# One expert item reordered, its gather in turned form, tables and a norm row loaded earlier, one refill in halves

## What is computed

```
h = x + token_mixer(rmsnorm(x), w_in, ..., w_out)    # attention, 8 heads; mLSTM, 4 heads
xt = rmsnorm(h, norm_ffn_w)
logits = xt @ w_router + b_router                    # 32 experts
top_val, top_idx = top_k(logits, 4); gate = softmax(top_val)
# for each expert e and the tokens that chose it (sorted into rows):
hdn = xb @ w_mlp1[e] + b_mlp1[e]                     # 1024 -> 2048
glu = min(hdn[:, :1024], 7); lin = clip(hdn[:, 1024:], -7, 7)
act = glu * sigmoid(1.702 * glu) * (lin + 1)
y = act @ w_mlp2[e] + b_mlp2[e]                      # 1024 -> 1024
out = rmsnorm(h + sum over 4 of gate * y, norm_final_w)
```

## Time and profile before

| | us |
|---|---|
| median of 3 runs | 1120.61 (1120.59 to 1120.95) |
| the profiled execution's own time | 1120.7 |
| its span, first to last instruction | 1118.7 |
| PE busy | 1081.9 (97%) |
| weight loads (PEld) busy | 485.3 (43%) |
| DVE busy | 368.2 (33%) |
| ACT busy | 246.9 (22%) |
| DMA | 439.15 MB, mean 393 GB/s |
| TensorE's granted clock | 0.998 of full speed |

### The profile page before, as it was taken

How to read it: one execution, slowest core, us unless ns; L and a number is a source line. 1 busy time by engine, 2 the same in 40 slices (tenths; PEclk the granted TensorE clock), 3 DMA queues, 4 the chain that set the end, 5 groups by cost and what they waited for, 6 DMA issues and landing times.

```text
span 1118.7 us, 14432 instructions
## 1 busy us (share of the span) xinstructions
PE 1081.9 (97%) x5393; PEld 485.3 (43%) x5394; DVE 368.2 (33%) x813; ACT 246.9 (22%) x346; POOL 3.0 (0%) x12
## 2 busy tenths in 40 slices
PE   9999999999999999999999999999999999999996
PEld 8888888533333333333333333333333333333332
DVE  6987786422222122222222222222222222222223
ACT  6745674311111111111111111111111111111112
POOL 0000000000000000000000000000000000000000
PEclk9999999999999999999999999999999999999999
DMA  9654479999999999999999999999999999999996
GB/s 337 230 186 152 151 221 421 427 412 427 428 428 435 431 429 432 433 430 432 432 431 396 431 431 432 433 433 433 431 431 431 433 431 431 431 431 431 424 424 277
DMA packets 38165, 439.15 MB, mean 393 GB/s; under 512 B 5276, under 2 KB 5464, under 8 KB 22424
## 3 DMA queue, kind: packets, MB, share of 16 engines
q1 hardware_dynamic: 37776, 437.78, 93.5%
q10 hardware_dynamic: 360, 0.95, 0.3%
HBM read 437.67 MB, written 1.05 MB: 392 GB/s over the span
## 4 chain that ended last, share of the span: by engine, by line
PE 80%; DMA 13%; DVE 6%; issue 1%; SPq 0%; ACT 0%; DVEq 0%; PEldq 0%
PE bank L1161 35%; PE bank L1190 18%; DMA ring<-in_w_mlp_dram 11%; PE bank L806 9%; PE bank L1088 3%; PE bank L1172 2%; PE bank L800 2%; DMA late_slots<-in_w_mlp_dram 2%; PE bank L968 2%; PE bank L1016 2%; DVE xn L1678 2%; DVE xn L1675 2%; DVE xn L1682 2%; PE bank L1064 1%; PE bank L1072 1%; PE bank L1138 1%
## 5 line engine op out<-in xcount | busy, mean ns | idle before, releaser
L1161 PE MATMUL bank<-ring,xn 128*64 128x512 f32 x1232 | 276.3, 595 | 6.3 <-DMA ring<-in_w_mlp_dram 6.3
L1161 PE MATMUL bank<-late_slots,xn 128*64 128x512 f32 x880 | 197.3, 595 | 3.6 <-DMA late_slots<-in_w_mlp_dram 3.5
L1161 PEld LDWEIGHTS bank<-ring,xn 128*64 128x64 f32 x1232 | 84.6, 136 | 163.6 <-issue 150.1
L1190 PE MATMUL bank<-ring,smo 128*64 128x512 f32 x624 | 138.3, 595 | 0.0
L713 ACT ACTIVATE xn<-bank 128x512 f32<-128x512 f32 x33 | 19.8, 599 | 479.9 <-PE bank L1161 479.9
L1161 PEld LDWEIGHTS bank<-late_slots,xn 128*64 128x64 f32 x880 | 60.4, 136 | 116.1 <-issue 106.5
L1691 DVE SCALAR_TENSOR_TENSOR moe_y_lo<-bank,st,moe_y_hi 128x512 fp32r<-128x512 f32 x33 | 24.8, 751 | 235.9 <-ACT moe_y_hi L720 235.9
L1675 DVE TENSOR_SCALAR xn<-bank 128x512 f32<-128x512 f32 x33 | 22.8, 692 | 219.4 <-PE bank L1161 219.4
L1190 PE MATMUL bank<-late_slots,smo 128*64 128x512 f32 x416 | 92.4, 595 | 0.2 <-DMA late_slots<-in_w_mlp_dram 0.2
L1190 PEld LDWEIGHTS bank<-ring,smo 128*64 128x64 f32 x624 | 43.0, 137 | 81.0 <-issue 81.0
L720 ACT ACTIVATE moe_y_hi<-bank,st 128x512 fp32r<-128x512 f32 x33 | 22.7, 687 | 234.1 <-PE bank L1190 234.1
(11 more groups left out here) (271 smaller groups left out, 886.3 us busy)
## 6 DMA issues: line engine op xcount, KB each, us to landing
ring<-in_w_mlp_dram SPq DMA_DIRECT2D x43, 4096.0 KB, 30.2
late_slots<-in_w_mlp_dram SPq DMA_DIRECT2D x29, 4096.0 KB, 27.8
ring<-in_w_mlp_dram SPq DMA_DIRECT2D x28, 2048.0 KB, 13.2
late_slots<-in_w_mlp_dram SPq DMA_DIRECT2D x15, 2048.0 KB, 15.3
ring<-in_w_in_dram SPq DMA_DIRECT2D x22, 1024.0 KB, 5.6
late_slots<-in_w_mlp_dram SPq DMA_DIRECT2D x6, 1024.0 KB, 35.9
ring<-in_w_branch_dram SPq DMA_DIRECT2D x4, 1024.0 KB, 5.0
ring<-in_w_out_dram SPq DMA_DIRECT2D x4, 1024.0 KB, 7.3
```

The costliest lines, as they stand in the source:

```text
L1161: last = mm(B[4 + u][g * C:(g + 1) * C, :], xgT[:, k % 4, k // 4, :], by_group(held[k // 2][0][:, k % 2, u * FF:(u + 1) * FF], g), start=F ...
L1190: last = mm(B[7][g * C:(g + 1) * C, :], actT[:, j, h * C:(h + 1) * C], held[4 + h][0][:, j // 2, (j % 2) * D + g * N:(j % 2) * D + (g + 1) ...
```

## The change

- Gather in turned form: x's columns are now the stationary operand (128 tokens by 128 features, every fourth feature), and the one-hot matrix the moving one (64 columns), so that the result comes out turned; 16 matmuls instead of 4. ACT's copy and `turn_rows` go.
- The expert item: in the last chunk of mlp1 both glu halves come first, and the new counter `glu_done` lets ACT's sigmoid and DVE's product of sigmoid and glu start before the linear half is done. DVE then clips the linear part and multiplies. `slots_used` goes up by 1 per slot instead of 2 per chunk.
- The one-hot matrix that is turned (`own`) and the identity beside it (`turner`) are bf16; the gates stand beside the identity in three bf16 pieces, made once by five DVE steps.
- b_mlp2 is issued by ACT after the copy of the slice mv, b_mlp1 and the final norm's row after the second softmax; the row has its own place in SBUF, over constants that are used no more. The constants are reordered for that.
- The first refill chunk that goes to place 0 is loaded in two halves, each when its slot is free.
- SP's wait ahead of the last quarter of w_out names `hi_used` in place of `slots_used`.

```diff
                 for t in range(TT):
                     pe.wait_ge(onehot, ready - 1 + t)
-                    for g in range(2):
-                        last = mm(B[6][g * C:(g + 1) * C, :], oneh[:, t, :], xs[:, t, g * N:(g + 1) * N],
-                                  start=(t == 0), stop=(t == TT - 1), skip_group_check=True)
+                    for j in range(ROWS):
+                        for g in range(2):
+                            rows_of = xs[:, t, g * N:(g + 1) * N].rearrange("p (q s) -> p s q", s=ROWS)[:, j, :]
+                            last = mm(B[6][:, (2 * j + g) * C:(2 * j + g + 1) * C], rows_of, oneh[:, t, :],
+                                      start=(t == 0 and j == 0 and g == 0), stop=(t == TT - 1), skip_group_check=True)
                 last.then_inc(gath, 1)
...
+                wide = P + TT * PIECES
                 for t in range(TT):
-                    last = mm(B[7][:, t * (P + TT):(t + 1) * (P + TT)], gated[:, t, :], cst[:, K_ID:K_ID + P + TT],
-                              start=True, stop=True)
+                    last = mm(B[7][:, t * wide:(t + 1) * wide], own[:, t, :], turner[:, :], start=True, stop=True)
                 last.then_inc(gt_turned, 1)
-
-            def turn_rows(ready):
-
-                pe.wait_ge(xg_out, ready)
-                for j in range(4):
-                    last = nc.tensor.transpose(B[6][:, j * P:(j + 1) * P], xg[:, j * P:(j + 1) * P], ident)
-                last.then_inc(xg_turned, 1)
...
+                def mlp1(k, u):
+                    for g in range(2):
+                        last = mm(B[4 + u][g * C:(g + 1) * C, :], xgT[:, k % 4, k // 4, :],
+                                  by_group(held[k // 2][0][:, k % 2, u * FF:(u + 1) * FF], g),
+                                  start=False, stop=(k == KB - 1), skip_group_check=True)
+                    return last
...
+                    mlp1(2 * c, 0)
+                    mlp1(2 * c, 1).then_inc(slots_used, 1)
+                    if c in in_pieces:
+                        pe.wait_ge(*in_pieces[c])
+                    mlp1(2 * c + 1, 0)
+                    mlp1(2 * c + 1, 1).then_inc(slots_used, 1)
+                pe.wait_ge(held[3][1], held[3][2])
+                mlp1(KB - 2, 0)
+                if 3 in in_pieces:
+                    pe.wait_ge(*in_pieces[3])
+                mlp1(KB - 1, 0).then_inc(glu_done, 1)
+                mlp1(KB - 2, 1)
+                if 3 in in_halves:
+                    pe.wait_ge(*in_halves[3])
+                mlp1(KB - 1, 1).then_inc(slots_used, 2)
                 gather(2 * i + 4)
...
-                turn_rows(i + 2)
                 pe.wait_ge(actT_a, i + 1)
 ...
             with act.Fori(0, items) as i:
-                act.wait_ge(slots_used, i * PER_EXPERT + (Q_MOE + KB))
+                act.wait_ge(glu_done, i + 1)
                 nc.scalar.activation(sig, B[4][:, :], ACT.Sigmoid, scale=ALPHA).then_inc(sig_ready, 1)
-                take_xg(i + 2)
                 act.wait_ge(turned_b, i + 1)
 ...
+                dve.wait_ge(sig_ready, i + 1)
+                v.tensor_scalar(sig, sig, SIG_TOP, None, ALU.min).then_inc(act_step, 1)
+                dve.wait_ge(act_step, 3 * i + 1)
+                v.scalar_tensor_tensor(out=lin, in0=B[4][:, :], scalar=LIMIT, in1=sig, op0=ALU.min, op1=ALU.mult)\
+                 .then_inc(act_step, 1)
                 dve.wait_ge(slots_used, i * PER_EXPERT + (Q_MOE + KB))
-                v.tensor_scalar(lin, B[5][:, :], LIMIT + 1.0, 1.0 - LIMIT, ALU.min, ALU.max).then_inc(lin_ready, 1)
...
+                v.tensor_scalar(B[5][:, :], B[5][:, :], LIMIT + 1.0, 1.0 - LIMIT, ALU.min, ALU.max).then_inc(act_step, 1)
+                dve.wait_ge(act_step, 3 * i + 3)
                 for j in (0, 2):
...
+                    v.tensor_tensor(actv.rearrange("p (s q) -> p q s", s=ROWS)[:, :, j:j + 2],
+                                    B[5][:, :].rearrange("p (q s) -> p q s", s=ROWS)[:, :, j:j + 2],
+                                    lin.rearrange("p (q s) -> p q s", s=ROWS)[:, :, j:j + 2], ALU.mult).then_inc(act_ready, 1)
 ...
+            v.tensor_copy(gate3[:, :, :, 0], gate[:, :, :]).then_inc(count_step, 1)
+            dve.wait_ge(count_step, 11)
+            v.tensor_tensor(gate_rest[:, :, :], gate[:, :, :], gate3[:, :, :, 0], ALU.subtract).then_inc(count_step, 1)
 ...
+            act.wait_ge(scored, AH)
+            for part in range(PIECES):
+                act.dma_start(b1raw[part * E:(part + 1) * E, :], b_mlp1[0]).then_inc(b1_in, 16)
+            act.dma_start(wfin[:, :], norm_final_w.rearrange("(a d) -> a d", a=1).broadcast_to([P, D])).then_inc(s_small2, 16)
             split(22)
...
+                elif CHUNKS * e + i == HALVED:
+                    for k in range(2):
+                        sp.wait_ge(slots_used, after * PER_EXPERT + (Q_MOE - PER_EXPERT + k + 1))
+                        sp.dma_start(places[place][:, k, :], src[:, k * SLOT:(k + 1) * SLOT]).then_inc(place_landed[place], 16)
...
-                sp.wait_ge(slots_used, min(Q_OUT + j - MIX_RING + 1, Q_BRANCH))
+                if j < 3:
+                    sp.wait_ge(slots_used, Q_OUT + j - MIX_RING + 1)
+                else:
+                    sp.wait_ge(hi_used, Q_BRANCH)
```

More of the change, by code:

```diff
@@ L123, in landings @@
             continue
-        counts[place] += 1
+        counts[place] += 2 if m == HALVED else 1
         table.append((place, counts[place]))
@@ L243, in build @@
         ohT = nc.alloc_sbuf_tensor_at("one_hot_T", [P, TT, P], F32R, offset=hm_at + 4 * S)
+        own = nc.alloc_sbuf_tensor_at("own_slots", [P, TT, P], BF16, offset=hm_at + 4 * 3 * S)
+        turner = nc.alloc_sbuf_tensor_at("ident_and_gates", [P, P + TT * PIECES], BF16, offset=hm_at + 4 * 3 * S + 2 * TT * P)
         b2t = sb("b2t", [P, N])
@@ L433, in _ @@
             for i in range(CHUNKS - 1):
-                wait_freed(after, i)
                 m = PLACES + 1 + i
+                if m != HALVED:
+                    wait_freed(after, i)
                 load(m // CHUNKS, m % CHUNKS, i)
@@ L746, in _ @@
             mm = nc.tensor.matmul
-            tables = cst[:, K_MASK:K_MASK + S]
+            tables = cst[:, K_LOWER:K_LOWER + S]
             def keep_warm(n, table, idle=B[7][:, 0:S]):
@@ L1142, in item @@
                 pe.wait_ge(xg_ready, i + 1)
-                for k in range(KB):
-                    if k == 2:
+                def mlp1(k, u):
+                    for g in range(2):
+                        last = mm(B[4 + u][g * C:(g + 1) * C, :], xgT[:, k % 4, k // 4, :],
+                                  by_group(held[k // 2][0][:, k % 2, u * FF:(u + 1) * FF], g),
+                                  start=False, stop=(k == KB - 1), skip_group_check=True)
+                    return last
+                for c in range(3):
+                    if c == 1:
                         pe.wait_ge(gT_ready, i + 1)
@@ L1150, in item @@
                         scatter(y_lo)
-                    if k == 4:
+                    if c == 2:
                         turn_gates(3 * i + 5)
-                    if k % 2 == 0:
-                        pe.wait_ge(held[k // 2][1], held[k // 2][2])
-                    elif k // 2 in in_pieces:
-                        pe.wait_ge(*in_pieces[k // 2])
-                    for u in range(2):
-                        if u and k == KB - 1 and 3 in in_halves:
-                            pe.wait_ge(*in_halves[3])
-                        for g in range(2):
-                            last = mm(B[4 + u][g * C:(g + 1) * C, :], xgT[:, k % 4, k // 4, :],
-                                      by_group(held[k // 2][0][:, k % 2, u * FF:(u + 1) * FF], g),
-                                      start=False, stop=(k == KB - 1), skip_group_check=True)
-                    if k % 2:
-                        last.then_inc(slots_used, 2)
+                    pe.wait_ge(held[c][1], held[c][2])
+                    mlp1(2 * c, 0)
[13 more added lines that the diff above has]
+                mlp1(KB - 1, 1).then_inc(slots_used, 2)
                 gather(2 * i + 4)
@@ L1558, in _ @@
                     v.memset(ohT[:, :, :].bitcast(F32), 0.0).then_inc(gated_zero, 1)
+                    v.tensor_copy(turner[:, 0:P], ident).then_inc(gated_zero, 1)
                 if n == 0:
@@ L1658, in _ @@
                 for t in range(TT):
-                    v.tensor_scalar(gated[:, t, :].rearrange("p (g s) -> p g s", g=2),
+                    v.tensor_scalar(own[:, t, :].rearrange("p (g s) -> p g s", g=2),
                                     places.unsqueeze(1).broadcast_to([P, 2, C]), at[t], None, ALU.is_equal)\
                      .then_inc(gated_ready, 1)
-                v.tensor_copy(cst[:, K_GATE:K_GATE + TT], gate[:, :, bass.ds(e, 1)].rearrange("p t a -> p (t a)"))\
-                 .then_inc(gated_ready, 1)
+                v.tensor_copy(turner[:, P:P + TT * PIECES].rearrange("p (t c) -> p t c", c=PIECES),
```

(8 more changed lines are left out.)

63 lines of the change are left out of this document (29 added, 34 removed).

## The result

The changed kernel takes 1334.45 us (median of 4 runs, 1324.23 to 1340.04) against 1120.78 for the kernel before on the same chip: a ratio of 1.189 (95% interval 1.185 to 1.193). The direction was forecast; the forecast of 1132.5 is 202 us too low, and its range ended at 1141. The profiled execution took 1339.21 us, its span 1337.3.

A forecast was written before the change was run, and what follows sets the result against it. The prediction took the later of two clocks, DMA transfers or PE, to bound the kernel. PE's 0.5 + 33 x 0.71 - 11.7 = +12.2 us on 1120.7 gave 1132.9, rounded to 1132.5; range 1117 to 1141.

The forecast's parts named there:

- Price of a pair, strided: Turned gather: each f32 pair of weight load and matmul costs 0.11 us, 32 pairs per item.
- rival C: Gather: reading every fourth column as weights is slower, 0.12 to 0.13 us a pair; about +25 us, 1146; chance 0.08.
- d: Expert item: its added length, +0.71 us forecast; 32p - 2.81, with p the time of one pair in the gather.
- The clock is no part of it: Whole kernel: TensorE ran at its full 2.4 GHz in every window, so clock speed was given no cost.
- the way from the gather's end to mlp2: Expert item: activation transposes, their copy and a semaphore before mlp2's first load, 0.95 us.
- One-hot turning: Expert item: turning the one-hots in bf16 instead of f32 saves 0.27 us, bounds 0.2 and 0.45.
- DVE's work after the last chunk: End of mlp1: clip and product, some 1.2 us, lie hidden under the gather's 3.4 us.
- s: First expert item: its start comes 0.5 us later, bounds 0 to 1.2.
- Two clocks: Kernel's end: the later of transfers (s + 14d, +10.4 us) and PE (s + 33d - 11.7, +12.2 us) decides.
- Order of chunk 3: Last chunk of mlp1: glu-first order and earlier sigmoid change the item by 0 us.
- Rival A: Gather: loads hidden, a pair costs 0.05 to 0.08 us, kernel faster at 1117.5 us; chance 0.14.
- B: Expert item: terms cancel, a pair at 0.085 to 0.09 us, kernel at 1121 us; chance 0.06.

The follow-up runs named there:

- e1: The changed kernel with 128 neighbouring columns of x as the gather's weights instead of every fourth; 1132.71 us, ratio 1.0101.
- e4: The changed kernel with the old gather back (4 matmuls, ACT's row copy, row transposes), the rest of the change kept; 1119.51 us, ratio 0.9986.
- e10: The changed kernel with contiguous gather weights and the gather done in two passes of 32 moving columns each; 1405.33 us.
- e8: The changed kernel with the gather's weights read at steps of 12, 24 and 16 bytes, the last from two starting points; 1314.72 us.
- e3: The changed kernel with strided weights kept, but 256 moving columns instead of 64 behind each load; 1306.67 us.
- e9: The changed kernel with contiguous gather weights and the gather done twice over, 64 pairs with 64 moving columns each; 1279.81 us.
- e2: The changed kernel with the gather's four weight sources read at steps of 4, 8, 16 and 32 bytes; 1248.34 us.
- e5: The kernel before with only the turned gather put in, its weights read at every fourth column; 1354.71 us.

## Why the prediction was wrong, by its steps

**Price of a pair, strided: the step that failed.** It was taken from loads of contiguous columns and carried over to a read that "as weights is in no row". That was rival C, and C had its mechanism right and its price wrong: 0.12 to 0.13 us where it is 0.239. No row bounded it from above, so the cost had to be called open, with both ends kept for the range; a range that ended at 1141, a pair of 0.118 us, had no ground. By the prediction's own d = 32p - 2.81, p = 0.239 gives d = 4.84, and PE's clock 0.5 + 33 x 4.84 - 11.7 = +148.5: 1269. The section of the Trainium skill quoted above spoke for C with its two hits in a line and against C with f32 strided by 4 for free, and the prediction weighed neither. Its remark that this stride costs nothing as moving operand has no row either: no matmul of the kernel before moves every fourth column. The gather moves 512 neighbours, and mlp1 moves four neighbours and skips four.

**"The clock is no part of it": failed for the changed kernel.** It was true of the rows of before and was never asked of the new gather. Against e1, the changed kernel's span is 206.6 us longer: 34 gathers x (7.66 - 3.71) = 134 for the loads; 33 x (8.70 - 7.09 for mlp2, + 0.20 for the transposes) = 60 and 2 in the first chunk for the clock; 10.6 for the interruption, less 1.4 that e1 waits for a transfer. Together 205. So of the forecast's 202 us of error, the loads are about two thirds and the clock three tenths.

**The rest held in the main, as e1 shows.** Pair 0.116 (forecast 0.11), so 3.71 us for 32 instead of 3.52; the way from the gather's end to mlp2 0.74 (0.24 + 0.44 and two short gaps, forecast 0.95). One-hot turning 0.64 to 0.22, so -0.42 (forecast -0.27, inside its bounds). The gather's part is then 0.62 + 0.42 = +1.04 (forecast +0.98), d = 27.38 - 26.76 = 0.62 (0.71). DVE's work after the last chunk is covered: the activation's transposes follow the gather at once. The first mlp2 starts at 233.89 in e1 and at 232.10 in the kernel before, so s = 1.79 - 0.62 = 1.2 (0.5 forecast, its bounds 0 to 1.2). PE waits for the first one-hots, which DVE begins at 221.50 instead of 219.29, 2.2 us later and not 1.4: the gather itself begins 0.5 later (208.85 against 208.38), so that its result is multiplied 0.9 later, and the five gate steps add 1.3.

**Two clocks.** PE's: 1.2 + 33 x 0.62 - 11.7 = +10.0; with a wait of 1.4 us for a transfer at 1047.6 us, 1132.1, and e1's profiled execution took 1132.49. That the forecast's 1132.5 lies 0.2 us from e1's median is in part luck: d was 0.09 us an item too high, 3 us, and s 0.7 and the wait 1.4 too low. (The point from which PE's clock counts is d = 11.7 / 19 = 0.62, not 0.59, so at e1's d the two clocks lie within 0.1 us of each other before that wait.) The sign of it was forecast too, a long pause of the transfers about 600 us; the window of e1:

```profile
600.00:610.00 10.00, 10.00 (x51) 3.36 (x48) 2.41 (x9) 1.15 (x1) 0.00 (x0) 1.00 0.21 62
```

**Order of chunk 3, put at 0:** right under the turned gather. With the old gather it isn't: e4's item is 0.82 us shorter, 0.42 of it from the one-hots and the other 0.4 about the size of PE's wait for DVE in the kernel before (14.7 us in 33 waits, 0.45 each).

**Rival A** (loads hidden, 0.05 to 0.08 us a pair) fell: even contiguous, a pair takes 0.116 us, 3.71 us for the gather. **B** fell with it.

## What to carry to other kernels

Before turning a matmul round, ask for the byte step at which the new weights are read; here 12 bytes or more were slow in f32. Data in order once, outside the loop, would take that away, but wasn't run as a kernel, and e1 says what to expect of it here: 1132.7 at best, while the old gather with the rest of the change has 1119.5. How a moving operand fares at such a step no run shows. A price from a row holds only for the access pattern of that row; where the pattern is new, keep the range open upwards. And when a stretch of dense matmuls is replaced by one of many loads with little moving behind them, look at the granted clock of that stretch and of the one after it, for the dense part behind pays as well.

## What the runs showed beyond that

- Weight loads of 128 f32 columns: 195 ns at 4 bytes, 201 at 8, 276 at 12, 316 at 24, 325 to 335 at 16 and 32, as means over stretches at both clocks. At the half clock contiguous loads take 332 ns instead of 192 (e10); those at 16 bytes stay at 329.
- The loops over expert items are sometimes interrupted: all of PE stands still between two items though nothing that the profile shows is missing. Chain of waits of the changed kernel:

```profile
944.35 7.88 PE bank L1201 x32
952.23 4.80 issue
...
958.94 2.53 issue
```

From that mlp2 to the next it is 43.8 us, 10.6 more than an item. This happens once in the changed kernel and in e8, three times in e3 (11 to 13 us each), four times in e9 (5 to 8 us each), and not in the kernel before, e1, e2, e4 or e5. e10 has four short stops of PE, 1.3 to 2.0 us. The queue of kind "instruction" moves 22 packets in the kernel before, 24 in e1 and e5, 33 in the changed kernel and e8, 51 in e3 and 63 in e9 and e10: 9 or 10 more with each interruption. So code seems to be fetched again there, which is argued from these counts and not shown. The clock falls behind it (0.50 from 570 to 580 us in e3). What brings it about was not tested; neither strided loads (e5 has them and no interruption) nor their absence (e9) decides it.
